# Sparse mixer of a two-block transformer kernel: head-pair transfers sent ahead of the weights, query tiles last, compression scores inside the short score units, first norm passes and root one stage earlier

## What is computed

```
def layer_norm(x, g, b):
    y = (xf - mu) * lax.rsqrt(var + LN_EPS) * g + b

def second_block(...):
    for i in range(DEPTH_2):
        h = gla_mixer(...) if i % 2 == 0 else nsa_mixer(...)
        x = layer_norm(DN_ALPHA * x + h, ln_g[i, 0], ln_b[i, 0])
        f = moe_ffn(...)
        x = layer_norm(DN_ALPHA * x + f, ln_g[i, 1], ln_b[i, 1])

def nsa_mixer(...):
    q, kc, vc, ks, vs, kw, vw, gates = split(x @ w_in)
    k_cmp = partial_rope(compress(kv_heads(kc), ...), cmp_end)   # 31 compressed keys
    v_cmp = compress(kv_heads(vc), ...)
    p_cmp = masked_softmax(q @ k_cmp, cmask)
    o_cmp = p_cmp @ v_cmp
    ...   # selected and windowed attention: with 512 tokens both see all earlier tokens
    o = gates[0] * o_cmp + gates[1] * o_slc + gates[2] * o_win

def moe_ffn(...):
    s = sigmoid(xt @ w_router); the best group of 4 of 16 experts, the best 2 in it
    h = silu(x @ w_gate[e]) * (x @ w_up[e]) * gate; out = h @ w_down[e]
```

## Time and profile before

| | us |
|---|---|
| median of 3 runs | 2192.19 (2191.56 to 2192.81) |
| the profiled execution, its own time | 2189.66 |
| its span, first to last instruction | 2187.8 |
| gated linear attention ends, first MoE begins | 1156 |
| sparse mixer: projection | 1477 to 1610 |
| compression | 1620 to 1642 |
| attention | 1643 to 1875 |
| second MoE, then the last norm | to 2174, to 2188 |

### The profile page before, as it was taken

How to read it: one execution, slowest core, us unless ns; L and a number is a source line. 1 busy time by engine, 2 the same in 40 slices (tenths; PEclk the granted TensorE clock), 3 DMA queues, 4 the chain that set the end, 5 groups by cost and what they waited for, 6 DMA issues and landing times. The chain is left out here.

```text
span 2187.8 us, 29543 instructions
## 1 busy us (share of the span) xinstructions
PE 1989.5 (91%) x11864; PEld 1654.0 (76%) x11864; DVE 1359.1 (62%) x1896; ACT 956.5 (44%) x1405; POOL 146.9 (7%) x209
## 2 busy tenths in 40 slices
PE   5998997988999999899996999959978999799996
PEld 5888887977999878687675888847766667678884
DVE  7974553626554455532438999874506773789997
ACT  5563335321110100433437777742114884577773
POOL 3442000000000000000012000100000000200010
PEclk9999998998999999999997999989997999799998
DMA  7433111314232122232043999942260001299993
GB/s 216 110 76 107 59 59 39 117 49 97 78 111 82 59 96 78 84 96 77 32 152 119 406 390 381 389 138 81 94 161 3 21 21 59 87 359 391 387 386 145
DMA packets 176327, 322.37 MB, mean 147 GB/s; under 512 B 46736, under 2 KB 112976, under 8 KB 176192
## 3 DMA queue, kind: packets, MB, share of 16 engines
q1 hardware_dynamic: 148464, 282.92, 37.1%
q0 software_dynamic: 11488, 31.28, 4.4%
q10 hardware_dynamic: 16240, 6.29, 1.1%
HBM read 299.41 MB, written 17.89 MB: 145 GB/s over the span
## 5 line engine op out<-in xcount | busy, mean ns | idle before, releaser
L2289 PE MATMUL ps<-m_ws,m_xbT 128*128 128x512 f32 x1344 | 314.5, 390 | 0.0
L2289 PEld LDWEIGHTS ps<-m_ws,m_xbT 128*128 128x128 f32 x1344 | 251.9, 188 | 52.1
L2520 DVE TENSOR_TENSOR m_ws<-ring,m_ws 128x2048 fp32r<-128x2048 f32 x112 | 256.1, 2289 | 28.6 <-ACT m_ws L2369 23.3
L1630 PE MATMUL ps<-ffT,ff_ws 128*128 128x264 f32 (+1 forms) x1056 | 241.6, 324 | 4.4 <-DVE ff_ws L433 4.4
L2369 ACT CAST m_ws<-ring 128x2048 fp32r<-128x2048 f32 x112 | 213.0, 1906 | 36.4 <-PE ps L2331 29.8
L1630 PEld LDWEIGHTS ps<-ffT,ff_ws 128*128 128x128 f32 x1056 | 176.8, 190 | 20.2 <-DVE ff_ws L433 4.5
L1630 PE MATMUL ps<-ffT_lo,ff_ws 128*128 128x264 f32 (+1 forms) x528 | 170.3, 322 | 0.0
L2331 PE MATMUL ps<-m_ws,m_hT 128*128 128x512 f32 x672 | 167.2, 398 | 0.0
L2517 DVE TENSOR_TENSOR m_ws<-ring,m_ws 128x2048 fp32r<-128x2048 f32 x56 | 128.2, 2289 | 20.2 <-ACT m_ws L2367 20.2
L2331 PEld LDWEIGHTS ps<-m_ws,m_hT 128*128 128x128 f32 x672 | 122.2, 188 | 23.6
L460 PE MATMUL ps<-fd_ws,fd_xs 128*128 128x512 f32 x528 | 121.9, 393 | 6.7 <-DVE fd_xs L433 6.7
(11 more groups left out here) (550 smaller groups left out, 4087.8 us busy)
## 6 DMA issues: line engine op xcount, KB each, us to landing
ring<-in_moe_w_gate SPq DMA_DIRECT2D x112, 512.0 KB, 5.6
ring<-in_moe_w_up SPq DMA_DIRECT2D x112, 512.0 KB, 7.4
ring<-in_moe_w_down SPq DMA_DIRECT2D x56, 1024.0 KB, 8.0
ring<-in_w_up SPq DMA_DIRECT2D x22, 1024.0 KB, 5.0
ring<-in_w_in SPq DMA_DIRECT2D x16, 1024.0 KB, 6.6
ring<-in_gla_w_in SPq DMA_DIRECT2D x12, 1024.0 KB, 5.3
ring<-in_w_down SPq DMA_DIRECT2D x11, 1024.0 KB, 6.2
ring<-in_nsa_w_in SPq DMA_DIRECT2D x10, 1024.0 KB, 7.9
```

The lines of the kernel that those rows point to most:

```text
L1630: ins = nc.tensor.matmul(ps[:, bank, 0:b - a], w[j][:, k, s * P:(s + 1) * P], x[l][:, k, a:b], start=(k == 0 and j == l), stop=(k == KD - ...
L2289: ins = nc.tensor.matmul(ps[:, it % 2, :], xbT[:, blk % 2, a, 4 * half + k, :].bitcast(F32R), v[b][:, k, :], start=(half == 0 and k == 0 a ...
L2520: ins = V.tensor_tensor(o, x.rearrange("p (j k w) -> p j k w", k=4, j=2), x0, ALU.subtract)
```

## The change

- Weight order and tiles of the projection: the slabs of the compression's inputs and of the keys come first, the queries last. Tiles: 4 flat, 4 key, 8 query.
- SP in the projection: the 32 head-pair DMAs stand ahead of `W.send`.
- The causal mask, the compression's mask table and `anyb` are loaded by ACT in `nsa_compress`; DVE makes the bf16 copies and scales the gates there.
- The attention's compression scores no longer use bank 7 after units 0 to 7. For query tile c they are 16 matmuls in a row in the free columns 256:512 of the banks of units 2, 3, 6, 7 (`CT`). Their transposes ride with those of units 6, 7, 10, 11. Head pair 0 is completed at unit 16 instead of 12 (`product_of`).
- Root and first norm pass: `squares` ends with Ln and Exp; `centre_first` does (x - mean) * g for token tiles 0 and 1 at the end of the stage before.
- MoE front: `rest_x(2)` and `rest_x(3)` come after the slot has been made; the gather does its high halves for six banks first, then the low halves.

```diff
-        self.n_nq = self.fm_slabs(w, 0, 4)
         self.n_nkv = [self.fm_slabs(w, c, 1)[0] for c in (1024, 1280, 1536, 2048)]
+        self.n_nq = self.fm_slabs(w, 0, 4)
...
+        act.wait_ge(self.squared, TT * self.n_ln)
+        self.nc.scalar.activation(self.lst[:, 1], self.lst[:, 0], ACT.Ln, bias=self.lneps[:], scale=1 / D).then_inc(self.rooted, 1)
+        act.wait_ge(self.rooted, 2 * self.n_ln - 1)
+        self.nc.scalar.activation(self.lst[:, 2], self.lst[:, 1], ACT.Exp, scale=-0.5).then_inc(self.rooted, 1)
+
+    def centre(self, dve, link, gam, t):
+        x = self.h[:, t, :]
+        link(self.nc.vector.scalar_tensor_tensor(x, x, self.lst[:, 4, t:t + 1], gam, ALU.add, ALU.mult))
+
+    def centre_first(self, dve, link, gam):
+        dve.wait_ge(self.ln_in, 32 * self.n_ln)
+        for t in range(2):
+            dve.wait_ge(self.squared, TT * (self.n_ln - 1) + t + 1)
+            self.centre(dve, link, gam, t)
...
# moe_stage, PE
-                pe.wait_ge(rl_done, TT)
-                pe.wait_ge(hot, TT)
-                for k in range(KD):
-                    if k >= 6:
-                        pe.wait_ge(xp_out, k - 3)
+                pe.wait_ge(rh_done, TT)
+                pe.wait_ge(hot, TT)
+                for k in range(6):
+                    gathered(k, 0)
+                pe.wait_ge(rl_done, TT)
+                for k in range(6):
+                    gathered(k, 1)
+                for k in range(6, KD):
+                    pe.wait_ge(xp_out, k - 3)
...
# moe_stage, DVE
                 dve.wait_ge(g_done, 1)
-                rest_x(2)
-                rest_x(3)
-
                 dve.wait_ge(cum_done, 1)
...
                 V.tensor_copy(slot[:], slotf[:]).then_inc(slot_done, 1)
+                rest_x(2)
+                rest_x(3)
                 lo(1)
                 lo(2)
...
# nsa_project
-            tiles = [("rope", *x) for x in rope] + [("flat", *x) for x in flat] + [("rope", *x) for x in rope2]
+            tiles = [("flat", *x) for x in flat] + [("rope", *x) for x in rope2] + [("rope", *x) for x in rope]
...
             @block.sync
             def _(sp):
-                W.send(sp)
                 for kv in range(2):
                     sp.wait_ge(kc_out, 2 * kv + 2)
...
+                W.send(sp)
                 for j in range(2):
                     for i in range(2):
-                        sp.wait_ge(rope_done, 8 + 2 * j + i + 1)
+                        sp.wait_ge(rope_done, 2 * j + i + 1)
...
# nsa_compress
                 for to, frm in loads:
                     act.dma_start(to, frm).then_inc(loaded, 16)
+                for to, frm in tables:
+                    act.dma_start(to, frm).then_inc(t_loaded, 16)
...
+                V.tensor_copy(m["ib"][:], self.ident[:])
+                dve.wait_ge(t_loaded, 16 * len(tables))
+                V.tensor_copy(m["cb"][:], causal[:])
...
# nsa_attention, PE
-                pe.wait_ge(masked, 2)
...
                         if it >= 2:
                             pe.wait_ge(exped, 2 * (it - 1))
+                            if it - 2 in CT:
+                                pe.wait_ge(c_read, CT.index(it - 2) + 1)
...
+                        if it in CT:
+                            c = CT.index(it)
+                            for v in range(NH // 2):
+                                for e in range(2):
+                                    r = slice(64 * e, 64 * e + 64)
+                                    ins = nc.tensor.matmul(ps[:, 2 * (it % 2) + e, 256 + 32 * v:256 + 32 * v + NCMP],
+                                                           qT[r, v, P * c:P * (c + 1)], kcT[r, v // 2, :], start=True, stop=True)
                         ins.then_inc(s_done, 1)
...
+                            if n - 4 in CT:
+                                c = CT.index(n - 4)
+                                pe.wait_ge(c_scaled, c + 1)
```

More of the change, by code:

```diff
@@ L2110, in _ @@
                     S.lo(dve, q)
+                link(V.memset(self.lneps[:], LN_EPS))
                 link(V.memset(self.lst[:], 0.0))
@@ L2353, in _ @@
                     act.wait_ge(self.zeros_in, 16 * NB)
-                act.wait_ge(ones_set, 1)
-                act.wait_ge(squared, TT * n_ln)
-                link(nc.scalar.activation(lst[:, 1], lst[:, 0], ACT.Ln, bias=self.lneps[:], scale=1 / D))
-                nc.scalar.activation(lst[:, 2], lst[:, 1], ACT.Exp, scale=-0.5).then_inc(rs, 1)
                 def hi(q):
@@ L2731, in nsa @@
             m["pcT"] = sb(at, "npcT", [P, TT, NG, P])
+            m["cb"], m["ib"] = (sb(at, "n" + n, [P, P], mybir.dt.bfloat16) for n in ("cb", "ib"))
+            m["cmask"] = sb(at, "ncmask", [P, TT, NCMP])
             self.nsa_compress(m)
@@ L2921, in nsa_compress @@
                 "zeroed", "own")
+            causal = sb(ctx, "cm_causal", [P, P])
+            anyb = sb(ctx, "cm_any", [P, TT])
+            t_loaded = self.sem("cm_t_loaded")
+            tables = [(causal[:], self.const(2, "causal")), (m["cmask"][:], self.const(2, "cmpmask").rearrange("p (t n) -> p t n", t=TT)),
+                      (anyb[:], self.const(2, "cmpany"))]
             w2 = A["nsa_w_cmp_k2_2"][0].rearrange("(k p) d -> p k d", p=P)
@@ L3148, in _ @@
             def _(act):
-                for to, frm in loads:
-                    act.dma_start(to, frm).then_inc(c_loaded, 16)
-                act.dma_start(causal[:], self.const(2, "causal")).then_inc(loaded, 16)
                 for it in range(N + 7):
@@ L3167, in _ @@
                                                  accum_out=st[:, it % 4, 2 + e:3 + e]).then_inc(exped, 1)
-                    if it >= 2 and it % 2 == 0 and it < 2 + 2 * TT:
-                        i = it // 2 - 1
-                        act.wait_ge(c_shifted, i + 1)
-                        nc.scalar.activation(pc[i][:, :, 0:NCMP], pc[i][:, :, 0:NCMP], ACT.Exp).then_inc(c_exped, 1)
-                    if 2 * TT <= it < 3 * TT:
-                        i = it - 2 * TT
-                        act.wait_ge(c_turned, i + 1)
-                        nc.scalar.copy(pcT[:, i].rearrange("p g q -> p (g q)"), ps[:, 7, :]).then_inc(c_out, 1)
-                    n = it - 6
-                    if n >= 0 and n % PAIR == PAIR - 1:
-                        u = n // PAIR
+                    if it - 1 in CT:
+                        c = CT.index(it - 1)
+                        act.wait_ge(c_shifted, c + 1)
+                        nc.scalar.activation(pc[c][:, :, 0:NCMP], pc[c][:, :, 0:NCMP], ACT.Exp).then_inc(c_exped, 1)
+                    if it - 1 in product_of:
+                        u = product_of[it - 1]
                         act.wait_ge(o_done, u + 1)
@@ L3203, in _ @@
                         dve.wait_ge(s_done, it + 1)
+                        if it in CT:
+                            c = CT.index(it)
+                            x = pc[c][:, :, 0:NCMP]
+                            dve.wait_ge(c_zeroed, c + 1)
+                            for e in range(2):
+                                src = ps[:, 2 * (it % 2) + e, 256:512].rearrange("p (h n) -> p h n", n=32)
+                                ins = V.tensor_tensor(x.rearrange("p (h a) n -> p a h n", a=2)[:, e], src[:, :, 0:NCMP],
+                                                      cmask[:, c, :].unsqueeze(1).broadcast_to([P, NH // 2, NCMP]), ALU.add)
+                                if e:
+                                    ins.then_inc(c_read, 1)
+                                else:
+                                    link(ins)
+                            dve.wait_ge(c_read, c + 1)
                         V.tensor_reduce(st[:, it % 4, 0:2], ps[:, 2 * s:2 * s + 2, 0:nk], AX.X, ALU.max, negate=True)\
```

142 lines of the change are left out of this document (57 added, 85 removed).

## The result

The changed kernel takes **2161.28 us**, the median of 4 runs (2158.15 to 2163.82), beside 2192.07 us for the kernel before on the same chip (4 runs, 2191.56 to 2192.81): a ratio of 0.9859, 95% interval 0.9842 to 0.9876, some 31 us. Four more runs in a later set gave 2160.81; over all eight the median is 2161.3. The profiled execution took 2161.58 us, with a span of 2159.5. The sign of the forecast was right; the time, 2174.0 with a range of 2163 to 2184, was 12.7 us too high.

A forecast was written before the change was run, and what follows sets the result against it. PE, busy 91% of the span, was taken as the bound, with time won where it idles between stages or runs at low clock. 9.2 + 1.9 + 3.1 - 1.5 + 1.7 + 0.8 + 3.0 = 18.2 off 2192.19 gives 2174.0 us, range 2163 to 2184.

The forecast's parts named there:

- First 16 units: Attention, maximum of unit 0 to unit 16: narrow matmuls as many as before, only their place changes; net cost 1.5 us.
- The clock at units 6 and 7: Attention's units 6 and 7: the clock falls there for about 3 us of high-clock work; cost 3 us.
- Gap: Idle PE between projection and compression: head-pair DMAs issued ahead of the weights remove most of it; gain 9.2 us (8.3 to 9.7).
- Compression: Compression's first instructions: they run at the high clock instead of 0.50, taking half the time; gain 1.9 us (0 to 1.9).
- Attention's start: Start of the attention: PE starts with the barrier, no longer waiting for mask and copies; gain 3.1 us (2.5 to 3.3).
- Last norm: Norm at the kernel's end: two passes run ahead of the barrier, six after it; gain 1.7 us.
- norm ahead of the projection: Norm before the projection: passes moved up, with DVE partly waiting for PE's transposes and ACT's copies; gain 0.8 us (0 to 1.7).
- MoE fronts: Both MoE fronts: one-hot 1.6 to 1.9 us earlier, and PE's gather with it; gain 3.0 us for both (0.5 to 3.8).
- Rival A: Attention's start: it begins at the high clock, saving 9 us more and dropping the 1.5 cost; 2163.5 us, chance 0.13.
- B: Attention's units 2 to 9: narrow blocks keep the clock low, costing 8 us instead of 1.5; 2180.5 us, chance 0.22.
- C: Projection to compression: the gap stays, through key copies behind the weights or a late slab; 2185.1 us, chance 0.07.
- D: Attention's first 16 units: the clock stays low throughout, adding 34 us; slower, 2208 us, chance 0.03.

## Why the prediction was wrong

By its own steps, with the changes of the profiled execution:

- **First 16 units, forecast a net cost of 1.5, measured a gain of 11.1.** This is the step that failed, by 12.6 us, about the whole error. Its sentence was "The narrow matmuls are as many as before: 128 instructions, half at 0.21 and half at 0.124 us. What changes is their place." The order changed too: row halves by turns. 128 instructions at the prediction's prices are 64 x 0.21 + 64 x 0.124 = 21.4 us; in the new trace they take 2 x 3.63 + 2 x 1.97 = 11.2. That is 10.2 of the 11.1. By the starts, where two now share a place, it is 64 places fewer, half at 0.213 and half at 0.112 us, or 10.4. (The 0.124 was itself misread: the last record of the row lasts 0.27 us, not 0.1, so the starts are 0.113 apart. That is worth 0.7 us and did not decide.) The run with eight of a half in a row gives 9.8 us back, the attention's part alone brings 10.9.
- **The clock at units 6 and 7, forecast a fall for a cost of 3.** It did not come. With one half in a row it does come: both runs with that order were at 0.50 again around unit 7, for 13.6 and 17.1 us, while in none of the traced runs with the turned order did it fall between its rise and the end of the mixer. So the same wrong premise gave both errors.
- **Gap, forecast 9.2, measured 9.6**, and 9.4 us of the kernel's time given back when only the queue's order was undone. SyncE's list from 1496.4 to 1519.1 was worked out as 1496.6 to 1521.4.
- **Compression, forecast 1.9, measured 1.0.** The high clock at its head came, 48 instructions in 10.40 us at 1.00. But the fall now comes at 1627.2, inside the value product, whose 16 instructions take 2.98 us; in runs where it comes later they take 2.00, and the compression 18.5 us. The term lacked this.
- **Attention's start, forecast 3.1, measured 3.0**, and 2.95 back in the run with late tables.
- **Last norm, forecast 1.7, measured 1.8; norm ahead of the projection 0.8 and 0.8; norm passes at the fronts nothing and nothing.**
- **MoE fronts, forecast 3.0 for both, measured 3.9.** The gather's order gives 1.5 each; the rest moves with the clock at the gather, where the same kernel showed 37.6 and 38.9 us in two executions.
- **Rival A gave 2163.5, close to the result, by a mechanism that is not there**: the attention began at 0.50. Its price of 9 us was not tested; the run that made the attention begin at 1.00 held the clock for 5.5 us and gained 1.8. B, C and D did not happen. The range missed since no case allowed the narrow products themselves another price. The working had bounds for their clock and their place only.

## What to carry to other kernels

When a change rewrites a loop around instructions that it keeps, compare the order in which they use the array, not only their number and place: a price per instruction holds for the neighbours it was read among. Where products use half of the rows, it is worth trying to alternate between the halves, each half with its own bank; here it halved the price of narrow ones. Transfers that the next stage waits for belong ahead of weight slabs that block on ring slots, and idle TensorE stretches of 2 to 3 us can be worth filling: in the fronts it paid, in the compression the medians did not show it.

## What the runs showed of the hardware

- Narrow fp32 products on 64 rows (31 columns) start one at a time, every 0.112 us at 1.00 and 0.213 us at 0.50, when one row half comes in a row. With the halves by turns two start within 0.007 us, one of each half, at the same distance from pair to pair. Alternating the bank alone leaves the distance as it is (0.213 us at 0.50).
- The granted clock depends on that order too: in the same place it stayed at 1.00 with turned halves and fell to 0.50 for 13.6 us with eight of one half in a row, though PE counted as busy for all of that time in the second case. Groups of 16 between other work, as before the change, did not lower it (1.00 for the 20.2 us of the earlier trace rows).
- What time at 0.50 costs differs by place: 5.6 us less of it in the attention's first units gave 1.8 us, 17.1 and 10.2 us less in the two fronts gave 3.2 and 1.7 us.
